# Recurrence of a hybrid decoder layer: one kept inverse, turned by TensorE at each level, and level products between chunk rows and parity rows

## The reference: what is computed

```python
sa = einsum('bhvk,bhk->bhv', s, -kk_t)
s = s * w_t + sa[..., None] * (kk_t * a_t) + v_t[..., None] * k_t
y_t = einsum('bhvk,bhk->bhv', s, r_t)
```

## Time and profile before

| | |
|---|---|
| median of three runs | 3307.31 us |
| the profiled execution's own time | 3311.72 us |
| its span | 3309.9 us |
| TensorE matmul, busy | 3024.0 us (91%), 31005 instructions |
| VectorE, busy | 1326.3 us (40%) |
| ScalarE, busy | 1001.9 us (30%) |
| instruction queue q8 | 197 packets, 3.23 MB |

### The profile page before, as it was taken

How to read it: one execution, slowest core, us unless ns; L and a number is a source line. 1 busy time by engine, 2 the same in 40 slices (tenths; PEclk the granted TensorE clock), 3 DMA queues, 4 the chain that set the end, 5 groups by cost and what they waited for, 6 DMA issues and landing times. The chain is left out here.

```text
span 3309.9 us, 74705 instructions
## 1 busy us (share of the span) xinstructions
PE 3024.0 (91%) x31005; PEld 2044.5 (62%) x31006; DVE 1326.3 (40%) x3169; ACT 1001.9 (30%) x2063; POOL 306.5 (9%) x321
## 2 busy tenths in 40 slices
PE   5999999999978888889999979988999999999990
PEld 3676667766748788877777745545555555555540
DVE  3554445444434444437666466653111111111118
ACT  3354334533323233326545533330111111111102
POOL 0000000000000000103332000000110000001104
PEclk8999999999989999999999889998999999999995
DMA  6122221211121222227776484417767687676658
GB/s 247 64 105 85 86 95 69 93 56 42 61 89 49 57 66 62 62 65 231 228 203 161 105 269 148 132 37 259 273 243 278 235 280 239 244 280 235 201 192 318
DMA packets 287267, 516.77 MB, mean 156 GB/s; under 512 B 95026, under 2 KB 109234, under 8 KB 282916
## 3 DMA queue, kind: packets, MB, share of 16 engines
q1 hardware_dynamic: 245708, 390.43, 35.5%
q10 hardware_dynamic: 25128, 66.26, 6.4%
q0 software_dynamic: 16176, 56.37, 4.8%
HBM read 394.99 MB, written 118.01 MB: 155 GB/s over the span
## 5 line engine op out<-in xcount | busy, mean ns | idle before, releaser
L298 PE MATMUL proj_main_ps<-proj_xt,proj_w 128*128 128x257 f32 x1536 | 351.1, 381 | 0.0
L298 PEld LDWEIGHTS proj_main_ps<-proj_xt,proj_w 128*128 128x128 f32 x1536 | 289.7, 190 | 41.5
L2696 PE MATMUL moe_y_ps<-moe_w,moe_ht 128*64 128x512 f32 x1312 | 302.4, 603 | 3.2 <-ACT moe_ht L2735 3.2
L2453 PE MATMUL out_proj_ps<-out_w,out_ct 128*128 128x512 f32 x544 | 242.0, 598 | 5.1 <-DMA out_w<-in_w_out_dram 5.1
L363 PE MATMUL proj_main_ps<-proj_w,proj_xt 128*128 128x512 f32 x512 | 225.3, 593 | 0.0
L2746 ACT ACTIVATE moe_sg<-moe_gate 128x256 f32<-128x256 f32 x82 | 31.5, 384 | 535.2 <-PE moe_gate L2680 535.2
L2696 PEld LDWEIGHTS moe_y_ps<-moe_w,moe_ht 128*64 128x64 f32 x1312 | 87.6, 137 | 159.5 <-issue 156.1
L2782 DVE COPY moe_y<-moe_y_ps 128x512 f32<-128x512 f32 x82 | 56.7, 692 | 315.0 <-PE moe_y_ps L2696 315.0
L2453 PEld LDWEIGHTS out_proj_ps<-out_w,out_ct 128*128 128x128 f32 x544 | 101.8, 192 | 121.0 <-issue 121.0
L363 PEld LDWEIGHTS proj_main_ps<-proj_w,proj_xt 128*128 128x128 f32 x512 | 97.0, 190 | 108.6 <-issue 107.1
L1796 DVE CUSTOM_DVE_ANT_0 att_sc<-att_s_ps,ahead_mask 128x256 f32<-128x256 f32 (+1 forms) x384 | 117.3, 362 | 106.0 <-PE att_s_ps L1599 106.0
(11 more groups left out here) (406 smaller groups left out, 5324.2 us busy)
## 6 DMA issues: line engine op xcount, KB each, us to landing
moe_w<-in_expert_w_dram SPq DMA_DIRECT2D x64, 2048.0 KB, 9.4
kept_first_gate<-in_expert_w_dram SPq DMA_DIRECT2D x16, 2048.0 KB, 9.7
kept_first_up<-in_expert_w_dram SPq DMA_DIRECT2D x16, 2048.0 KB, 15.1
y_rows<-moe_y ACTq DMA_DIRECT2D x164, 128.0 KB, 6.1
ft_p<-proj_uf SPq DMA_DIRECT2D x32, 642.0 KB, 3.2
y_rows<-ahead_feat POOLq DMA_DIRECT2D x33, 512.0 KB, 6.0
rwkv_feat<-ft_p SPq DMA_DIRECT2D x48, 321.0 KB, 3.2
att_s_k<-in_cache_att_k_dram ACTq DMA_DIRECT2D x14, 1024.0 KB, 6.5
```

Source lines behind the costliest of these rows:

```text
L298: last = mm(out[:, 0:w + 1], W[:, k, kind * C + m * P:kind * C + (m + 1) * P], XT[n % 2][:, k, 0:w + 1], start=(k == 0), stop=(k == KT - 1))
L2453: last = mm(proj_ps[j][:], CT[t % 2][:, k, :], W[:, k, 512 * j:512 * (j + 1)], start=(k == 0), stop=(k == KT - 1))
L2696: last = mm(py[j * HB:(j + 1) * HB, :], HT[:, c, r * HB:(r + 1) * HB], W2[s][:, k, j * 512:(j + 1) * 512], start=(k == 0), stop=(k == FE / ...
```

## The change

The transpose is no longer kept beside the inverse. `T` becomes [128, 8, 64]. After the 16 products of `w`, TensorE also turns the current inverse with four full 128x128 transposes into the other half of the two banks of `level_ps`, and `w_copy` takes both banks (1024 columns) to `WZ`. The products of `w` now go from a chunk's rows to a parity's rows, those of `grow` back, so that each set uses four quadrants; the transpose is grown (in `WZ`) at the last level alone. `put` is 512 columns wide at each level, `begin` loses its two transposed copies, and `hg` and `values` use four quadrants. TensorE's and ScalarE's lists are put in another order; VectorE's list stays as it is.

```diff
-        T = ring("t", [P, H, P], 3)
-        W = sb("w", [P, H, DH])
+        T = ring("t", [P, H, DH], 3)
+        WZ = ring("w_turned", [P, 2, 512], 2)
...
             def w(i, l):
-                pe.wait_ge(t0, 3 * i + 3)
+                pe.wait_ge(t0, 2 * i + 2)
...
-                for h in range(H):
-                    for c in range(2):
-                        last = mm(level_ps[other(c), 0, h, :], NB[i % 3][part(c), h, 0:DH], T[i % 3][part(c), h, 0:DH],
-                                  start=True, stop=True, skip_group_check=True)
+                for q in range(4):
+                    for e in range(2):
+                        for c in range(2):
+                            mm(level_ps[part(e), c, q * DH:(q + 1) * DH], NB[i % 3][part(c), 2 * q + e, 0:DH], T[i % 3][part(c), 2 * q + e, :],
+                               start=True, stop=True, skip_group_check=True)
+                for q in range(4):
+                    last = nc.tensor.transpose(level_ps[:, q // 2, turned_at(q)], T[i % 3][:, 2 * q:2 * q + 2, :].rearrange("p e k -> p (e k)"), ident)
...
             def grow(i, l):
...
+                for q in range(4):
                     for c in range(2):
+                        for e in range(2):
+                            if l < levels_of(i):
+                                last = mm(level_ps[part(c), e, q * DH:(q + 1) * DH], z_of(x, e, q, c), w_of(x, e, c, q),
+                                          start=True, stop=True, skip_group_check=True)
+                            else:
+                                last = mm(z_of(level_ps, e, q, c), w_of(x, e, c, q), z_of(x, e, q, c),
+                                          start=True, stop=True, skip_group_check=True)
...
             def values(n):
-                pe.wait_ge(t0, 3 * n + 1)
+                pe.wait_ge(t0, 2 * n + 2)
...
+                            last = mm(head_ps[c][part(e), q * DH:(q + 1) * DH], KK[n % 3][part(c), 2 * q + e, 0:DH], U[n % 3][part(c), 2, 2 * q + e, :],
...
             def hg(n):
...
+                            last = mm(tail_ps[e][part(c), q * P:(q + 1) * P], z_of(WZ[n % 2], e, q, c), UE[n % 3][part(e), :, q, c, :],
...
                 if tail:
-                    parts(i - 1)
+                    parts_qm(i - 1)
                 if longer:
                     w(i, 3)
+                if tail:
+                    parts_state(i - 1)
+                if longer:
+                    grow(i, 3)
                 if head:
                     b_products(i + 1)
                 if longer:
-                    grow(i, 3)
+                    w(i, 4)
                 if tail:
                     y_inside(i - 1)
                 if longer:
-                    w(i, 4)
+                    grow(i, 4)
                 if head:
                     k_products(i + 1)
                 if longer:
-                    grow(i, 4)
+                    w(i, 5)
                 if tail:
                     step(i - 1, 0)
+                if longer:
+                    grow(i, 5)
                 if head:
                     n_products(i + 1)
-                if longer:
-                    w(i, 5)
+                if tail:
+                    step(i - 1, 1)
                 if head:
                     values(i + 1)
-                if longer:
-                    grow(i, 5)
-                if tail:
-                    step(i - 1, 1)
...
             def w_copy(i, l):
                 a.wait_ge(w_done, base(i) + l)
-                nc.scalar.copy(W[:], level_ps[:, 0]).then_inc(w_copied, 1)
+                nc.scalar.copy(WZ[i % 2][:], level_ps[:]).then_inc(w_copied, 1)
...
-                            last = nc.scalar.copy(U[n % 3][other(c), j].rearrange("p h k -> p (h k)"), head_ps[b][part(c), :])
+                            for e in range(2):
+                                last = nc.scalar.copy(UE[n % 3][part(e), 0, :, c, :], four(head_ps[b][part(c), :])[:, :, part(e)])
...
             def put(i, l):
                 v.wait_ge(g_done, base(i) + l)
+                if l < levels_of(i):
+                    block = level(l)[:, 0:DH].rearrange("p (e q k) -> p e q k", e=1, q=1).broadcast_to([P, 2, 4, DH])
+                    v.copy_predicated(by_parity(T[i % 3][:]), block.bitcast(U32), level_ps[:, :, 0:256].rearrange("p e (q k) -> p e q k", q=4)).then_inc(t_set, 1)
...
             def begin(n):
...
-                for c in range(2):
-                    block = level(0)[part(c), DH:P].rearrange("p (o k) -> p o k", o=1).broadcast_to([DH, H, DH])
-                    last = v.copy_predicated(T[n % 3][other(c), :, DH:P], block.bitcast(U32), NB[n % 3][part(c), :, 0:DH])
-                last.then_inc(t0, 1)
```

More of the change, by code:

```diff
@@ L935, in rwkv_chunks @@
         part = lambda c: slice(c * DH, (c + 1) * DH)
-        other = lambda c: part(1 - c)
+        w_of = lambda x, e, c, q: x[part(e), c, q * DH:(q + 1) * DH]
+        turned_at = lambda q: slice(256 + q % 2 * P, 256 + (q % 2 + 1) * P)
+        z_of = lambda x, e, q, c: x[part(e), q // 2, 256 + q % 2 * P + c * CH:256 + q % 2 * P + (c + 1) * CH]
         by_parity = lambda x: x.rearrange("p (q e) k -> p e q k", e=2)
@@ L1013, in _ @@
                 if n >= 3:
-                    for j in range(2):
-                        g.wait_ge(hg_done[j], n - 2)
-                nc.gpsimd.tensor_copy(T[n % 3][:], wide(eyes, H)).then_inc(t_init, 1)
+                    g.wait_ge(w_done, base(n - 2))
+                nc.gpsimd.tensor_copy(T[n % 3][:], wide(eyes[:, 0:DH], H)).then_inc(t_init, 1)
         @blk.tensor
@@ L1033, in grow @@
                 pe.wait_ge(w_copied, base(i) + l)
-                for h in range(H):
+                x = WZ[i % 2]
+                for q in range(4):
                     for c in range(2):
-                        if l < levels_of(i):
-                            mm(level_ps[part(c), 0, h, :], T[i % 3][other(c), h, DH:P], W[other(c), h, :],
-                               start=True, stop=True, skip_group_check=True)
-                    for c in range(2):
-                        last = mm(level_ps[other(c), 1, h, :], W[other(c), h, :], T[i % 3][other(c), h, DH:P],
-                                  start=True, stop=True, skip_group_check=True)
+                        for e in range(2):
[5 more added lines that the diff above has]
+                                          start=True, stop=True, skip_group_check=True)
                 last.then_inc(g_done, 1)
@@ L1100, in hg, with parts_qm @@
                     pe.wait_ge(y_copied, n)
[L1101 to L1105, removed]
+                for q in range(4):
+                    for c in range(2):
+                        for e in range(2):
+                            last = mm(tail_ps[e][part(c), q * P:(q + 1) * P], z_of(WZ[n % 2], e, q, c), UE[n % 3][part(e), :, q, c, :],
                                       start=True, stop=True, skip_group_check=True)
-                    last.then_inc(hg_done[g], 1)
-            def parts(n):
+                            if q == 3 and c == 1:
+                                last.then_inc(hg_done[e], 1)
+            def parts_qm(n):
                 u, x = U[n % 3], HG[n % 2]
@@ L1120, in parts, with parts_state @@
                             h = 2 * q + e
-                            mm(tail_ps[c][part(e), q * P + DH:(q + 1) * P], x[part(c), h, 0:DH], u[part(c), 1, h, :], start=True, stop=True, skip_group_check=True)
+                            last = mm(tail_ps[c][part(e), q * P + DH:(q + 1) * P], x[part(c), h, 0:DH], u[part(c), 0, h, :], start=True, stop=True, skip_group_check=True)
+                last.then_inc(qm_done, 1)
+            def parts_state(n):
+                u, x = U[n % 3], HG[n % 2]
                 if n >= 1:
@@ L1135, in parts @@
                             h = 2 * q + e
-                            last = mm(state_ps[c][part(e), q * DH:(q + 1) * DH], u[part(c), 2, h, :], u[part(c), 3, h, :], start=False, stop=False, skip_group_check=True)
-                last.then_inc(qm_done, 1)
+                            mm(state_ps[c][part(e), q * DH:(q + 1) * DH], u[part(c), 1, h, :], u[part(c), 2, h, :], start=False, stop=False, skip_group_check=True)
             def y_inside(n):
@@ L1150, in y_inside @@
                             h = 2 * q + e
-                            last = mm(tail_ps[e][part(c), q * DH:(q + 1) * DH], KK[n % 3][part(c), h, DH:P], u[part(c), 3, h, :], start=False, stop=False, skip_group_check=True)
+                            last = mm(tail_ps[e][part(c), q * DH:(q + 1) * DH], KK[n % 3][part(c), h, DH:P], u[part(c), 2, h, :], start=False, stop=False, skip_group_check=True)
                 last.then_inc(y_begun, 1)
@@ L1261, in rows @@
                         for c in range(2):
-                            last = nc.scalar.copy(U[n % 3][other(c), j].rearrange("p h k -> p (h k)"), head_ps[b][part(c), :])
+                            for e in range(2):
```

(17 more changed lines are left out.)

28 lines of the change are left out of this document (15 added, 13 removed).

## The result

The changed kernel is slower: 3341.4 us (median of 7 runs, 3326.0 to 3354.9) against 3312.6 (7 runs, 3303.2 to 3321.8); the ratio is 1.0104, interval 1.008 to 1.0129. The forecast was 3315, a change within 0.3% of the kernel before, and the range 3298 to 3334, so the time lies 7 us above the range. The profiled execution took 3351.97 us, its span 3350.2.

What follows compares the result with a forecast made beforehand. TensorE's instruction page supply was taken to nearly set the pass. Terms of +13, +3, +0.7, -5.7 and -2.8 made +8 us: profiled 3311.7 to 3320, median 3307.3 to 3315; range 3298 to 3334.

Steps and rivals of the forecast that it cites:

- the fourth rival: TensorE's clock falls in waits of 2.2 us and it runs at 1.2 GHz for a while; chance called small.
- first pass: First tile's pass of the recurrence: 25.8 us against 22.8, the new waits in full, +3 us.
- The two new waits: TensorE idles before w 4 and w 5 for VectorE's puts 3 and 4: 2.15 to 2.2 us each, +4.4 a pass.
- fourteen passes: Full passes of the recurrence after the first: 28.3 us each, +0.9 a pass, +13 us in all.
- pass into the sample tiles: The recurrence's pass into the first sample tile: +0.7 us.
- three sample passes: Passes without put 3 or 4, so no new wait: 16.9 us against 18.8 each, -5.7 us in all.
- drain at the end: The drain at the end gets shorter: -2.8 us.
- Pages: TensorE's instructions load in pages of about 254 records; waits for late pages fall from 3.5 to about 1.4 us a pass.
- Unabsorbed page waits: Page lateness stays at 0.6 us a page despite the new waits: 30.6 us a pass, 3347 in all; chance 0.13.
- rival 1: Slower: w's two-bank copy takes 1.17 us, not 1.01: +16, 3323 us; chance 0.28, shared with more drain between quadrant and full-array work.
- rival 2: Faster: TensorE's instruction pages arrive in time, so a pass takes 26.9 us and the sum is -17, 3290 us; chance 0.12.
- Rival 3: Faster: VectorE's puts 3 and 4 go ahead of the masked copies, pass 24 us, 3255 in all; chance almost nothing.

Runs made afterwards that it cites:

- both waits filled: The changed kernel with four unused 256-column products between b and w 4, and four between k and w 5: 3319.8 us, ratio 1.003 to the kernel before.
- fewer records: The kernel before without grow's transposed products at levels 2 to 4 (needed work left out, a price only): 3270.2 us, ratio 0.9866.
- half filled: The changed kernel with two unused 256-column products in each of the two waits: 3319.3 us, ratio 1.0044 to the kernel before.

## Why the prediction was wrong

- *The step that failed: the fourth rival, and with it a clock term of nothing in the sum.* "The clock falls ... Small" was wrong. I argued from one wait of 1.72 us in the first pass of the kernel before. There, products ran for 3 us behind each of the waits of 1.50 and 1.72 us (976.57 to 979.56 and 981.28 to 984.26). After the change, sets are half as long: 1.3 to 1.6 us of products stand between the first waits, and the waits reach 2.13 us. That the shorter sets matter is my reading; the runs vary the waits, and none varies the sets alone. The clock cost 22.5 us, which with the 10.4 of the next point makes the +33 of the profiled recurrence (7.6 more lie in the attention stage, on unchanged code, and are not explained). The sign of being wrong that the prediction named, a clock under 0.95, is met in the first pass (0.73).
- *The two new waits* were right: 2.15 to 2.2 forecast, measured 59.6 / 28 = 2.13. So were the copy (1.01), w (1.25, measured 1.27 from 1210.13 to 1211.40) and grow (0.65 and 0.69).
- *The rest of the sum was near by luck in part.* At full clock, in the kernel with both waits filled, the recurrence is 531.3 - 520.9 = 10.4 us longer than before, and the sum had 8 (the kernel before has 10 us of low clock in its fourteen passes itself). Its terms miss in both directions:

| term | forecast | both waits filled |
|---|---|---|
| fourteen passes | +13 | +8.3 (28.0 a pass, 28.3 forecast) |
| first pass | +3 | +3.0 (25.8, as forecast) |
| pass into the sample tiles | +0.7 | +1.9 |
| three sample passes | -5.7 | -1.8 |
| drain at the end | -2.8 | -1.3 |
| before the first copy | 0 | +0.3 |

- *Pages.* 1.4 us a pass were expected and 0.8 came (0.6 at full clock), while the chain was 0.5 longer than laid out. The supply itself was read rightly (fewer records). Unabsorbed page waits (in rival 1) and pages wholly in time (rival 2) are both out, nearer to rival 2. Rival 2's own price was added up wrongly: 28.3 to 26.9 is 1.4 us in each of fourteen passes, which takes +8 to about -12, or 3296, and not to -17.
- *Sample passes.* 16.9 were expected, 18.0 came. `values` now fills both head banks, so `given` waits for `c_copy`, which I had not priced (2.4 of the missing 3.3 us in three passes). The -5.7 also counts from a laid-out 18.8, while the earlier trace rows give 18.5; measured it is -1.6.
- *Rival 1*, the dearer copy, is out. *Rival 3* was the kernel that should have been built: 3255 was its price, 3273 the measured one.

## What to carry to other kernels

When an operation is moved on one engine's list, lay the other engines' lists beside it: an in-order engine that meets the moved one's consumer first holds up all behind it. If a change adds regular waits to TensorE and shortens the work between them, price the clock too: filling the waits with unused products is a quick way to measure it. Count instruction records as a resource where products are small.

## What was not expected of the hardware

TensorE's clock fell with two waits of about 2.1 us in a 29 us pass (38 us at 1.2 GHz in 409). In the same fourteen passes it did not fall when 1.1 us (half filled) or 2.0 us (filled) of useless products stood in each wait. In the seven runs of the kernel after, longer times go with lower mean clocks, from 3326.0 us at 0.963 to 3354.9 at 0.952, so a good part of their spread is probably that of the clock.
